# A decoder block on one Trainium2 core: small loads on another queue, an earlier turn of the vectors, and another order of the last round

## What is computed

```python
h = rms_norm(x, g_mix)
z = h @ w_in + b_in            # conv a and b, q, k, v, two gates: 5376 columns
y_conv = silu(layer_norm(conv31(a * sigmoid(b)) + conv_b)) @ w_conv_out + b_conv_out
y_attn = window_attention(q, k, v, sinks) @ w_attn_out + b_attn_out
x = x + (sigmoid(gate_conv) * y_conv + sigmoid(gate_attn) * y_attn) @ w_out
h = rms_norm(x, g_ffn)
# top 4 of 32 experts for each token, weights by a softmax of the 4 logits
g = minimum(h @ w_gate[e] + b_gate[e], 7);  u = clip(h @ w_up[e] + b_up[e], -7, 7)
x = x + sum over e of weight[e] * (((u + 1) * g * sigmoid(1.702 * g)) @ w_down[e] + b_down[e])
out = rms_norm(x, g_final)
```

## Time and profile before

| What | Value |
|---|---|
| Runs | 1176.33, 1176.87, 1177.09 us; median 1176.87 |
| The profiled execution's own time | 1177.35 us |
| Its span, first to last instruction | 1175.6 us, mean granted clock 0.996 |
| TensorE busy | 1123.7 us, 96% of the span |
| VectorE, ScalarE, GpSimd busy | 28%, 15%, 4% |
| Expert products (L1447), TensorE | 2080 records at 594 ns and 992 at 593 ns |
| Projections (L1193), TensorE | 928 records at 381 ns |
| Read from HBM | 440.08 MB, 375 GB/s over the span |
| DMA rate in slices 1 to 10 of 40 | 267, 349, 219, 179, 143, 72, 251, 250, 215, 333 GB/s |
| DMA rate in slices 11 to 39 | 423 to 435 GB/s |
| Chain that ended last | TensorE 82%, VectorE 6%, DMA 4%, issue 4% |

### The profile page before, as it was taken

One profiled execution on the slowest core, in us unless ns is written; L12 is line 12 of the kernel. 1 busy time (PEld: TensorE's weight loads), 2 busy tenths in 40 slices (PEclk: granted clock), 3 DMA queues, 4 the chain that ended last, 5 costly groups with the idle time before them and its releaser, 6 DMA issues.

```text
span 1175.6 us, 13690 instructions
## 1 busy us (share of the span) xinstructions
PE 1123.7 (96%) x5333; PEld 532.8 (45%) x5333; DVE 326.1 (28%) x793; ACT 179.6 (15%) x351; POOL 47.6 (4%) x39
## 2 busy tenths in 40 slices
PE   8999799999999999999999999999999999999997
PEld 7888687865333333333333333333333333333332
DVE  1899964224111111111111121121111111111111
ACT  2111266123011010010010110010000000000011
POOL 2560000000000000000000000000000000000000
PEclk9999999999999999999999999999999999999999
DMA  8966416659999999999999999999999999999996
GB/s 267 349 219 179 143 72 251 250 215 333 423 423 428 434 430 431 431 431 433 430 433 431 433 431 430 433 431 433 431 431 431 434 431 430 431 431 435 433 423 259
DMA packets 54134, 441.69 MB, mean 376 GB/s; under 512 B 4184, under 2 KB 34138, under 8 KB 37337
## 3 DMA queue, kind: packets, MB, share of 16 engines
q1 hardware_dynamic: 53512, 440.20, 90.4%
q0 software_dynamic: 432, 0.95, 0.4%
q10 hardware_dynamic: 160, 0.13, 0.0%
HBM read 440.08 MB, written 1.05 MB: 375 GB/s over the span
## 4 chain that ended last, share of the span: by engine, by line
PE 82%; DVE 6%; DMA 4%; issue 4%; another core or an unknown queue 2%; DVEq 1%; ACT 0%; ACTq 0%
PE bank L1447 54%; PE bank L1193 8%; PE bank L1415 5%; DVE arena L822 4%; PE bank L1400 4%; DMA arena<-in_w_down 4%; PE bank L1311 2%; PE bank L1483 2%; PE bank L1454 1%; PE bank L1407 1%; PE bank L1490 1%; DVEq L821 1%; PE bank L1343 1%; PE bank L1216 1%
## 5 line engine op out<-in xcount | busy, mean ns | idle before, releaser
L1447 PE MATMUL bank<-arena,x_columns 128*64 128x512 f32 x2080 | 467.7, 594 | 21.1 <-DMA arena<-in_w_up 19.7
L1447 PEld LDWEIGHTS bank<-arena,x_columns 128*64 128x64 f32 x2080 | 149.7, 137 | 293.4 <-issue 272.7
L1447 PE MATMUL bank<-arena,act_columns 128*64 128x512 f32 x992 | 219.1, 593 | 9.3 <-DMA arena<-in_w_down 9.3
L1193 PE MATMUL bank<-arena 128*128 128x256 f32 x928 | 204.2, 381 | 1.1 <-DVE arena L789 1.1
L1193 PEld LDWEIGHTS bank<-arena 128*128 128x128 f32 x928 | 175.8, 191 | 27.0 <-issue 1.8
L1447 PEld LDWEIGHTS bank<-arena,act_columns 128*64 128x64 f32 x992 | 76.4, 137 | 148.2 <-issue 148.2
L822 DVE SCALAR_TENSOR_TENSOR arena<-arena x240 | 97.3, 484 | 0.1
L1047 DVE TENSOR_SCALAR bias_selector<-ones_bf,expert_onehot 96x64 bf16<-96x64 bf16 x32 | 7.6, 237 | 268.7 <-PE bank L1407 268.7
L1081 DVE TENSOR_SCALAR gate_clipped<-bank 128x512 f32<-128x512 f32 x32 | 22.1, 692 | 202.7 <-PE bank L1447 202.7
L1085 DVE TENSOR_SCALAR hidden<-bank 128x512 f32<-128x512 f32 x32 | 22.1, 691 | 181.6 <-PE bank L1447 181.6
L1415 PE MATMUL bank<-y_block,scatter 64*128 64x512 f32 x248 | 61.5, 614 | 0.0
(11 more groups left out here) (192 smaller groups left out, 498.6 us busy)
## 6 DMA issues: line engine op xcount, KB each, us to landing
arena<-in_w_up SPq DMA_DIRECT2D x25, 4096.0 KB, 44.7
arena<-in_w_down SPq DMA_DIRECT2D x25, 4096.0 KB, 45.9
arena<-in_w_gate SPq DMA_DIRECT2D x24, 4096.0 KB, 43.5
arena<-in_w_in SPq DMA_DIRECT2D x21, 1024.0 KB, 11.8
arena<-in_w_gate SPq DMA_DIRECT2D x10, 2048.0 KB, 12.1
arena<-in_w_up SPq DMA_DIRECT2D x9, 2048.0 KB, 11.6
arena<-in_w_down SPq DMA_DIRECT2D x8, 2048.0 KB, 15.2
arena<-in_w_down SPq DMA_DIRECT2D x11, 1024.0 KB, 8.6
```

Source lines behind the costliest of these rows:

```text
L1193: last = pe.matmul(bank[n % 3][:, j * T:(j + 1) * T], w[:, c, j * P:(j + 1) * P], src[:, c, :], start=(c == 0), stop=(c == C - 1))
L1447: last = pe.matmul(dst[h * CAP:(h + 1) * CAP, :], lhs(row), cols(rows[:, row, :], h), start=(row == 0), stop=(row == MROWS - 1))
```

## The change

Small loads. SyncE no longer issues the seven vectors, conv_w and the router's weights between pieces 1 and 2. ScalarE issues the vectors and conv_w after it has copied the two norm rows, and the router's weights after the vectors are turned.

The start of TensorE. The row product of tile 0 comes ahead of the turns of tile 1, that of tile 1 after half of these; VectorE's first four chunks wait for that half only. The vectors are turned after projection 0, conv_w after projection 1.

The last round. The last three matrices are down 30, up 31, down 31 (before: up 31, down 30, down 31); their parts are cut anew. TensorE does gate 31, down 30, up 31, loads the count of blocks, scatters 30 whole, turns, and does down 31. The extra buffers are gone.

The final norm. One half (1, 1) is gained early instead of two; VectorE turns the first half's sum of squares into a bias, and ScalarE's root takes the second half's sum with that bias, so the sums aren't added.

```diff
-    if n == NM - 1:
-        return NE - 1, 2
+    if n >= NM - 3:
+        return ((NE - 2, 2), (NE - 1, 1), (NE - 1, 2))[n - (NM - 3)]
...
-ROW_PARTS[NM - 1] = [(0, 4), (4, 6), (6, 7), (7, 8)]
+ROW_PARTS[NM - 2] = [(0, 4), (4, 6), (6, 7), (7, 8)]
+ROW_PARTS[NM - 1] = [(0, 2), (2, 4), (4, 6), (6, 7), (7, 8)]
...
-                if n == 1:
-                    for name, (row, rows) in VEC.items():
-                        if name != "g_mix":
-                            sp.dma_start(vrows[row:row + rows, :],
-                                         t_in[name].rearrange("(c p) -> c p", p=P)).then_inc(vecs_loaded, 16)
-                    sp.dma_start(cwrows, t_in["conv_w"]).then_inc(cw_loaded, 16)
-                    sp.dma_start(wrt, t_in["w_router"].rearrange("(c p) e -> p c e", p=P)).then_inc(wrt_loaded, 16)
...
+            for name, (row, rows) in VEC.items():
+                if name != "g_mix":
+                    act.dma_start(vrows[row:row + rows, :], t_in[name].rearrange("(c p) -> c p", p=P)).then_inc(vecs_loaded, 16)
+            act.dma_start(cwrows, t_in["conv_w"]).then_inc(cw_loaded, 16)
+
             act.wait_ge(vecs_out, 2)
+            act.dma_start(wrt, t_in["w_router"].rearrange("(c p) e -> p c e", p=P)).then_inc(wrt_loaded, 16)
...
                 if y_before:
-                    copy_y(b * MPE + (FRONT - LEAD + MPE))
+                    copy_y(b * MPE + (FRONT - LEAD + MPE) if then_gather else FRONT + EW * (NM - 2))
...
             def y_std(t):
                 act.wait_ge(squares_dve, t + 1)
-                act.activation(std[:, 0, t:t + 1], ss[:, 1, t:t + 1], ACT.Sqrt, scale=1.0 / D,
-                               bias=eps[:, 0:1]).then_inc(stds, 1)
+                act.wait_ge(squares, TT + 2 * t + 2)
+                act.activation(std[:, 0, t:t + 1], ss[:, 3, t:t + 1], ACT.Sqrt, scale=1.0 / D,
+                               bias=ss[:, 1, t:t + 1]).then_inc(stds, 1)
             square(0, 0)
             square(0, 1)
+            y_std(0)
             square(1, 0)
-            y_std(0)
-            act.wait_ge(gain_on, 2)
+            act.wait_ge(gain_on, 1)
             square(1, 1)
...
-            dv.wait_ge(xTp, TT)
             dv.wait_ge(row_out, TT)
             for c in range(C):
+                if c % (C // 2) == 0:
+                    dv.wait_ge(xTp, 2 + c // (C // 2))
...
-            dv.wait_ge(squares, TT + 1)
-            gained(0, 0)
-            sum_of_squares(0)
+            mean_of_half(0)
             dv.wait_ge(y_done, 2 * TT)
             gained(1, 1)
             y_rstd(0)
-            dv.wait_ge(rstd_ready, 1)
-            dv.wait_ge(gain_on, 1)
-            dv.tensor_scalar(ysum[:, 0, 0:512], ysum[:, 0, 0:512], rstd[:, 0, 0:1], None, ALU.mult).then_inc(ysum_ready, 1)
+            half_out(0, 0)
+            mean_of_half(1)
             half_out(0, 1)
-            sum_of_squares(1)
             y_rstd(1)
             half_out(1, 0)
...
+            x_columns(0, range(C))
+            pe.wait_ge(gmix_loaded, 16)
+            pe.transpose(bank[1][:, 0:C], vrows[0:C, :], ident[0:C, 0:C]).then_inc(gmixT, 1)
+            rstd_to_row(0)
+            x_columns(1, range(C // 2))
+            rstd_to_row(1)
+            x_columns(1, range(C // 2, C))
...
             project(0, hT, ready=hT_ready, ready_by=1)
-            project(1, hT, (0,))
             pe.wait_ge(vecs_loaded, 16 * (len(VEC) - 1))
             pe.wait_ge(vecs_out, 1)
             pe.transpose(bank[6][:, 0:VROWS], vrows, ident[0:VROWS, 0:VROWS]).then_inc(vecsT, 1)
-            project(1, hT, (1,))
-            project(2, hT)
+            project(1, hT)
             pe.wait_ge(cw_loaded, 16)
...
-            for n in range(3, GATE0 + 1):
+            for n in range(2, GATE0 + 1):
...
             gate_product(b, NM - 4)
+            down_product(b - 1, NM - 3)
             pe.wait_ge(swT_out, b)
-            up_product(NM - 3)
-            down_product(b - 1, NM - 2, dst=G, halves=(0,))
+            up_product(NM - 2)
+            pe.wait_ge(n_ready, 1)
+            n_blocks = pe.value_load(nblk_i[0:1, 0:1], min_val=NE, max_val=NBLK)
+            pe.wait_ge(yb_out, b)
+            scatter()
             turn_act(b)
             turn_weights(b)
-            down_product(b - 1, NM - 2, dst=G, halves=(1,))
-            pe.wait_ge(yb_out, b)
-            scatter((0,), swT_late, y_late)
-            down_product(b, NM - 1, columns=act_late)
-            scatter((1,), swT_late, y_late)
+            down_product(b, NM - 1)
```

More of the change, by code:

```diff
@@ L701, in copy_xg, with copy_y, moe_block @@
                 act.activation(xg, G[:], ACT.Copy).then_inc(xg_out, 1)
-            def copy_y(done, src=DN, dst=yb):
+            def copy_y(done):
                 act.wait_ge(piece_done, done)
-                act.activation(dst, src[:], ACT.Copy).then_inc(yb_out, 1)
-            def moe_block(b, then_gather=True, y_before=True, y_after=False, sw=swT, columns=actT):
+                act.activation(yb, DN[:], ACT.Copy).then_inc(yb_out, 1)
+            def moe_block(b, then_gather=True, y_before=True, y_after=False):
                 act.wait_ge(gmin_ready, b + 1)
@@ L726, in _ @@
                 moe_block(b)
-            moe_block(NE - 2, sw=swT_late)
-            moe_block(NE - 1, then_gather=False, y_before=False, columns=act_late)
-            copy_y(FRONT + EW * (NM - 1), G, y_late)
+            moe_block(NE - 2)
+            moe_block(NE - 1, then_gather=False)
             copy_y(FRONT + EW * NM)
@@ L1083, in moe_block @@
                 dv.tensor_tensor(gmin, gmin, sig, ALU.mult).then_inc(act_steps, 1)
-                dv.wait_ge(piece_done, b * MPE + (FRONT - lead + 2 * EW))
+                dv.wait_ge(piece_done, b * MPE + (FRONT - lead + 2 * EW) if then_gather else FRONT + EW * (NM - 1))
                 dv.tensor_scalar(uclip, B[:], LIMIT, -LIMIT, ALU.min, ALU.max).then_inc(act_steps, 1)
@@ L1123, in _, with mean_of_half @@
                         moe_block(b, lead=0)
-            def sum_of_squares(t):
-                dv.wait_ge(squares, TT + 2 * t + 2)
-                dv.tensor_tensor(ss[:, 1, t:t + 1], ss[:, 2, t:t + 1], ss[:, 3, t:t + 1], ALU.add).then_inc(squares_dve, 1)
+            def mean_of_half(t):
+                dv.wait_ge(squares, TT + 2 * t + 1)
+                dv.tensor_scalar(ss[:, 1, t:t + 1], ss[:, 2, t:t + 1], 1.0 / D, EPS, ALU.mult, ALU.add).then_inc(squares_dve, 1)
             def y_rstd(t):
@@ L1162, in _, with x_columns @@
             pe.wait_ge(consts, 2)
-            for t in range(TT):
+            def x_columns(t, chunks):
                 pe.wait_ge(x_loaded[t], 16)
-                for c in range(C):
+                for c in chunks:
                     cols = slice(c % 2 * T + t * P, c % 2 * T + (t + 1) * P)
@@ L1169, in _, with rstd_to_row @@
                 last.then_inc(xTp, 1)
-                if t == 0:
-                    pe.wait_ge(gmix_loaded, 16)
-                    pe.transpose(bank[1][:, 0:C], vrows[0:C, :], ident[0:C, 0:C]).then_inc(gmixT, 1)
-            pe.wait_ge(consts, 4)
-            for t in range(TT):
+            def rstd_to_row(t):
+                pe.wait_ge(consts, 4)
                 pe.wait_ge(diag_ready, t + 1)
                 pe.matmul(bank[ROW_BANKS[t]][:, 0:P], ones[:], diag[:, t, :], start=True, stop=True).then_inc(row_done, 1)
+            x_columns(0, range(C))
[5 more added lines that the diff above has]
+            x_columns(1, range(C // 2, C))
             def project(n, src, halves=(0, 1), ready=None, ready_by=4):
@@ L1408, in tokensT, with scatter @@
                 last.then_inc(xT_done, 1)
-            def scatter(tokens=range(TT), sw=swT, y=yb, ends=False):
-                for t in tokens:
+            def scatter(ends=False):
+                for t in range(TT):
                     for h in range(2):
                         rows = slice(h * CAP, (h + 1) * CAP)
-                        last = pe.matmul(Y[t][h][:], sw[rows, t, :], y[rows, :], start=False, stop=ends)
+                        last = pe.matmul(Y[t][h][:], swT[rows, t, :], yb[rows, :], start=False, stop=ends)
                         if ends:
@@ L1473, in up_product, with down_product @@
                 product(B, n, lambda c: xT[:, c % 4, c // 4, :], bup, cycle)
-            def down_product(b, n, cycle=None, dst=DN, halves=(0, 1), columns=actT):
+            def down_product(b, n, cycle=None):
                 pe.wait_ge(actT_out, b + 1)
-                product(dst, n, lambda c: columns[:, c % 4, c // 4, :], None, cycle, halves)
+                product(DN, n, lambda c: actT[:, c % 4, c // 4, :], None, cycle)
             def turn_act(b):
```

7 lines of the change are left out of this document (2 added, 5 removed).

## The result

| What | Before | After |
|---|---|---|
| Median (lowest to highest) | 1176.87 (1176.33 to 1178.25, 9 runs) | 1173.33 (1167.89 to 1174.68, 9 runs) |
| Profiled execution, its span | 1177.35, 1175.6 | 1173.97, 1172.2 |
| Mean granted clock of the profiled execution | 0.996 | 0.995 |

The ratio is 0.9946 with a 95% interval of 0.9924 to 0.9967: the kernel is faster, by 3.5 us between the two medians. The two measures differ: the ratio stands for 6.4 us (3.9 to 8.9), the medians of the runs shown give 0.9970 and their means 0.9962. The forecast was 9.8, beyond both. Seven of the nine runs lie between 1172.87 and 1174.68, at a mean clock of 0.994 or 0.995; the other two are at 1167.89 and 1167.93, at 0.999 and 0.998. These two are close to the forecast, 1167.1; the seven are something that it didn't have.

The account below looks back on a forecast made before the run. TensorE's progress bounds the kernel until about 260 us, then the expert DMA stream. Gains 6.2 + 2.9 + 0.4 + 0.3 = 9.8 us; 1177.35 - 9.8 - 0.48 = 1167.1 us, range 1165.3 to 1171.5.

Parts of the forecast that it names:

- faster by more than 0.2%: Whole kernel: faster by more than the 0.2%, 2.4 us, that a measurement can tell; chance 0.88.
- the late vectors: After the first projection: TensorE stalls 0 to 2.8 us for the vectors; 0.2 us lost was taken.
- The norm row: Kernel start: row products between the turns of x start the first projection earlier; gain 0.6 us (0.3 to 0.8).
- Small loads: Start, loads on ScalarE's queue: 0.2 us lost waiting for the vectors, no stall for conv_w.
- loads a little late: Rival, early projections: vectors or conv_w land 1 to 6 us late, giving 1168.1 to 1173 us; chance 0.12.
- the one-engine rule: conv_w's load: 31 rows run on one DMA engine, so another queue makes it no faster and the later arrival is likelier.
- Taps and standstill: Convolution to layer norm: taps start at 27.5, removing TensorE's standstill, gain 6.2 us, and its slow clock, gain 2.9 us.
- the second reading: GpSimd's second product beside the taps: blocked only until one instruction ends, done by 42 us, VectorE 0.9 us more in hand.
- that rival: VectorE stays late at the layer norm's sum: GpSimd's product costs 1 to 3 us, giving 1168 to 1170; chance 0.08.
- The end: Last round and final norm: gains of 0.4 us (1.0 to a loss of 0.7) and 0.3 us (0 to 0.6).
- All up to 260 us hangs on TensorE and moves by 9.1: Work before the expert stream: TensorE's time saved starts the stream earlier by as much, 9.1 us.
- the stream: Rival, expert stage: DMA binds from before 260 us, so only the end's 0.7 us stays, 1176.2; chance 0.06.

Follow-up runs that it names:

- experiment 8: Kernel before with early turns of vectors and conv_w and the norm rows between x's turns, small loads left on SyncE's queue: 1172.65 us, ratio 0.9951.
- the control: Kernel before plus four filler products in the router stage and the output sums' four starting products spread between down 0's rows: 1178.27 us, ratio 1.0005.
- the end alone: Kernel before with only the last round and final norm changed: 1176.48 us, ratio 0.9994.
- experiment 3: Changed kernel with one more wait, for ScalarE's square, ahead of the second scores, putting the standstill back: 1174.77 us, ratio 0.9987.
- one mend: Either the four router-stage filler products or the output sums' starting products spread between down 0's rows; in the changed kernel alone 1171.06 and 1170.26 us.
- the last control: Kernel before with twelve dummy products in the standstill, four router-stage filler products and the spread start of the output sums: 1177.54 us.
- the last kernel of experiment 8: Whole change with small loads left on SyncE's queue, plus router-stage filler and spread start of the output sums: 1168.67 us, ratio 0.9922.
- experiment 4: Changed kernel with four small filler products in TensorE's short router-stage waits ahead of the first expert: 1171.06 us, ratio 0.9942.
- experiment 2: Kernel before with twelve dummy products in TensorE's standstill ahead of the sum over partitions: 1181.65 us, ratio 1.0022.

## Why the prediction was right, and where it was wrong

The time, 1173.33, lies outside the range (1165.3 to 1171.5); 1170.5, which the ratio would make of 1176.87, lies inside it. The sign and "faster by more than 0.2%" came true. The terms' own far end was too near: 1170 leaves out the 2.8 us that the late vectors might cost by the working; with them it is 1172.3.

- *The norm row.* 0.6 us forecast, 0.51 measured (10.24 to 9.73). VectorE came at 8.90 (9.0 forecast); the first weight piece, called no hindrance, held TensorE for 0.39.
- *Small loads.* Issues of 0.27 to 0.65 us; the vectors cost nothing (0.2 forecast), conv_w 0.75 (nothing forecast, 0.1 at the far end of its bounds). This is the rival "loads a little late", just short of its low end. Of the two arrivals worked out for conv_w, 16.4 and 23.9, the later was the near one, as the one-engine rule had it, and the range of the term should have gone past it. That the queue is no help (experiment 8) was not asked in the prediction at all: its turns earlier would have worked with the loads where they stood.
- *Taps and standstill.* 28.50 for 27.5, late by the 0.75 and the piece's wait. The standstill and the slow clock behind it are gone as written: TensorE 8.35 ahead for 9.1; 0.75 + 0.1 less than forecast, 0.2 back from the vectors, 0.1 less from the clock (2.75 from the sum to the turns, for 2.9). GpSimd's product was shown for 8.77 us and not 15.42, so until 49.1, neither the 55.0 of the sum nor the 42 of the second reading, and VectorE came in time: that rival fell. Its "too short for the clock", for waits of 1 to 3 us, isn't shown by any run.
- *The end.* 0.7 forecast, 1.05 measured. Down 31 starts 1155.94 - 1120.87 = 35.07 us behind the wait of down 29, before 35.46: 0.4 gained, as computed; the norm takes 3.46 us from the first square to the last pair for 4.03, 0.57 for 0.3.
- *The failed step* is the sentence "All up to 260 us hangs on TensorE and moves by 9.1", with "inside the stream nothing counts until its last bytes" behind it. It took the granted clock as something that the change could only give back. The work from 260 us on had a clock of 1.00 in the trace of before, and the prediction took that for granted. It can't be: in the profiled run, and by their mean clock in six more of nine, the new kernel loses the clock there twice, 3.2 us up to the first expert and 2.8 more in the stream (5.16 to 2.34), of which 1.7 are the down product's own (8.78 for 7.09). With the clock kept, the sum holds: 9.3 us for the whole change against its control (9.8 forecast), and 9.3 for the start, on SyncE's queue and without a late load, in the profile of experiment 8 (9.1 forecast).
- *What stays open.* Why the kernel before keeps its clock at these places (from 276 to 326 us there) in most of its runs, and which of the work there lets it fall in the others. A slow stretch at 143 goes with that in every profile of before, of the end alone and of the control, and in four of six runs of experiment 3, but what links them isn't shown, and whether one mend would do isn't either. Of the 2.2 us that the last control lacks, its profile shows where most went and not why.

## What to carry to other kernels

Ahead of a prediction, look for stretches of thin work (few rows, few columns, small transposes) directly in front of long products, even where the granted clock is 1.00 now: removing a stall elsewhere went with its falling there (which part of that work matters isn't shown), and where TensorE's progress releases DMAs the loss is paid in bytes as well. Read the clock over the whole span of the new kernel before believing a saved microsecond lost to "the stream", and when the times of its runs fall in two groups, compare their mean clocks first. Here a few filler products and thin ones spread among full ones brought back 4 us (1173.3 to 1169.0); in the control, which had nothing to win, they cost 1.0 us in the profile and too little for the ratio (0.9993 to 1.0017).

## What the runs showed of the hardware that I had not expected

- The same program gets different clocks in different runs: 1167.9 us at 0.998 to 0.999 and 1172.9 to 1174.7 at 0.994 to 0.995. In these slow stretches TensorE was busy, not idle: 2.00 of 2.00 us in the windows at 269 and 313. What stood ahead of the first was 128x64 and 128x32 products and transposes, ahead of the second 32-row products.
- The first projections can be slow with a granted clock of 1.00 in the record: 12.41 us for 10.60 in the last control, 8.96 for 7.17 in the last kernel of experiment 8, 8.27 for 7.17 in experiment 4. In experiment 2 the same loss, 12.31 for 10.60, stands beside a recorded clock of 0.50 at 12 to 14 us, so the record may miss such a stretch. It is worth 1.1 to 1.8 us and stands in four of fourteen profiles, in kernels that don't touch this work too, so it widens every comparison of single profiles here.
- Closing the gap in the loads at 12 to 15 us was worth nothing: after moves 229 GB/s at 12 to 14 us, and experiment 8, which moves 70 there, is no slower.
